# Early starts for x, weight parts and turned rows in a two-block transformer kernel on one Trainium2 core

## The chip, the cores and the metric

The kernel runs on one core of a Trainium2 chip. The metric is the device time of one execution in microseconds; a kernel is run several times and the median counts. In the profile PE is TensorE, DVE is VectorE, ACT is ScalarE, POOL is GpSimd and SP is the engine that only issues DMAs. PEld is TensorE's weight load, which overlaps its matmuls.

## The reference

256 tokens of width 1024 pass through a first block of two layers and then through a second block. Layer 0 mixes with neighbourhood attention (8 heads) and latent attention (8 heads), layer 1 with dilated attention (16 heads in three groups); each is followed by a squared-ReLU MLP of width 4096. The second block mixes three branches (a gated linear recurrence, 8 causal heads, 4 heads over a memory) and ends with a gated feed-forward of width 3072. Cut to what matters:

```python
for layer in range(DEPTH):                      # DEPTH = 2
    xn = rms_norm(x, norm_mix[layer])
    x = x + (even_mixer if layer % 2 == 0 else odd_mixer)(xn, ...)
    x = x + sq_relu_mlp(rms_norm(x, norm_mlp[layer]), mlp_w1[layer], mlp_w2[layer])
x = rms_norm(x, norm_final)
# second block: xn = rms_norm(x, mix_norm_gain); h = xn @ w_in
# x = x + (sum over 3 branches of sigmoid(gate) * (branch @ w_branch)) @ w_out
# x = x + (gelu(conv(xn @ w_gate)) * (xn @ w_up)) @ w_down ; out = rms_norm(x)
```

## The kernel before

All work is written out by hand as one program per engine: the functions `tensor`, `scalar`, `vector`, `gpsimd` and `sync` each issue their engine's instructions in a fixed order, and named events (a semaphore and a count, `tell` and `at`) tie them together. An instruction that waits holds up everything behind it on its engine.

**Weights.** The plan lists 192 slabs of weights, mostly 1024 rows by 256 columns. `sync` loads slab n into `raw` (5 buffers) once the product of slab n-5 is done. Every fp32 product is made of three fp32r products, so each slab is split: ScalarE writes the high part `whi` (`high`, L985; 3 buffers, free again when the product of the slab three before it is done), and the low part `wlo = raw - whi` is written by VectorE (`low`, L1387) or, for slabs that `pooled` names, by GpSimd in four pieces (L2071). `ahead(n)` on each engine means: make the part of slab n+2. Activations are split in the same way: `XH`/`XL` for the normed x (`gained`), `OH`/`OL` for the attention output (`outputs`), `GH`/`GL` (parts of `HH`, `HL` in the profile) for the blended branches. TensorE multiplies hi by hi, lo by hi and hi by lo (L520, or L540 and L556, which go by chunks of x). Slab numbers: IN2 = 122, BLENDS = 134, OUT2 = 152 (two slabs of w_out by rows, 152 and 153, then two halves, 154 and 155), ODO = 86 (w_o of layer 1, slabs 86 to 89), and slab 90 is the first of the second MLP.

**The head.** `x` comes in as rows in two halves of 512 columns. TensorE transposes it in four chunks (`turn_in`, L592), VectorE copies each chunk from PSUM to `XT` (L1577), ScalarE scales it to `XH` (L1017), VectorE makes `XL` (L1425). The gain `mixgain` has its own small transpose (L742), and VectorE's queue copies its result before it copies x. `keep_busy(n)` (L736) issues n matmuls of ones for the clock of TensorE. Behind the chunks VectorE makes the low parts of slab 0 (`first_low`, L1567), slab 1, sums squares, and makes slab 2 (L1387).

**Attention.** Heads are units; stage s of `attend` starts the scores of unit s, and finishes the values of unit s-3 and the transposes of the probabilities of unit s-2. Outside layer 1's dilated heads two units go as a pair. VectorE takes the maxima, then `softmax` scales the exponentials in `SN` (L1474) for TensorE's transposes (L661), and `probs` copies turned rows from PSUM to `PT` (L1482, odd units; ScalarE does the even ones) for the value products (L690). In layer 0, stages 5 to 8 also turn the memory rows (`turn_in(("mem", ...))`), whose PSUM banks come free when `memory_low` has written the low parts `HL` (L1657). PSUM has 8 banks, handed out in turn, so a bank waits for the reader of its use 8 before.

**Between the stages.** At the end of layer 1's mixer, stage 34 yields the last `OL` (L1492); then slab 89 gives four pieces that VectorE adds to `XT` (`onto_natural`, L1517). The first chunk of the next product needs `XH` of the first piece. In the second block's input product VectorE computes two chained norms (`factors`), while ScalarE waits for them (`both mean`, L1255). In its last blend stage (s = 14) ScalarE writes the high parts of the four blended pieces (L1285) behind VectorE's sums (L1926, L1928, L1932).

## Time and profile before

| what | value |
|---|---|
| median of 3 runs | 1252.59 us (1250.91 to 1252.92) |
| the profiled execution's own time | 1252.58 us |
| its span, first to last instruction | 1250.8 us |
| TensorE busy | 1232.5 us, 99% of the span |
| VectorE busy | 819.0 us, 65% |
| ScalarE busy | 620.3 us, 50% |
| GpSimd busy | 275.0 us, 22% |
| granted clock of TensorE, mean | 0.996 |

The profiled execution lies within 0.01 us of the median, and 1.8 us are outside its span. Busy time of TensorE is so near the span that only its gaps and the stretches at a lower clock can be won back without taking work away. In a row of the timeline the columns are start and duration in us, engine, line, operation, output and inputs, number of instructions merged, and in brackets the idle time in front and what ended it.

### The profile page before, as it was taken

Reading aid. Unit: us, or ns where it says so; the run is one execution under the profiler, and the core shown is the slowest. Engines: PE = TensorE matmul, PEld = TensorE weight load, DVE = VectorE, ACT = ScalarE, POOL = GpSimd, SP = SyncE. Lnnn points to the kernel's source line nnn. Section 1 sums busy time; section 2 is a strip of 40 time slices with the busy share of each in tenths; the row PEclk is TensorE's granted clock in tenths of the full one; section 3 lists DMA queues with packets and bytes.
Section 4 is the critical chain, followed back from the end, with each engine's and each line's share of the span. In section 5 each row is a group of like instructions: output and inputs, shape, how many; then the busy total and the mean of one; then the engine's idle time right before and its main releaser. Section 6 shows DMA issues by size and latency. Waiting matters only on the chain.

```text
span 1250.8 us, 23346 instructions
## 1 busy us (share of the span) xinstructions
PE 1232.5 (99%) x10005; PEld 1188.4 (95%) x10005; DVE 819.0 (65%) x1093; ACT 620.3 (50%) x772; POOL 275.0 (22%) x208
## 2 busy tenths in 40 slices
PE   8999999999999999999999999999999999999998
PEld 8978899999999999999999999999999999999986
DVE  6778666655574667666877755497876467656643
ACT  5565455543344454545555553336566435444442
POOL 2500010000021202020310000289211476434100
PEclk9999999999999999999999999999999999999999
DMA  9542455555576555554355555555544455555551
GB/s 277 175 135 102 135 169 178 193 172 199 169 240 212 172 183 172 165 190 144 103 169 174 198 170 197 172 177 172 173 163 141 137 184 169 180 189 171 188 185 65
DMA packets 188693, 214.48 MB, mean 171 GB/s; under 512 B 5243, under 2 KB 170430, under 8 KB 188590
## 3 DMA queue, kind: packets, MB, share of 16 engines
q1 hardware_dynamic: 183182, 205.11, 50.3%
q10 hardware_dynamic: 5216, 7.42, 2.0%
q8 instruction: 79, 1.29, 0.4%
q0 software_dynamic: 192, 0.46, 0.1%
q14 instruction: 24, 0.20, 0.1%
HBM read 205.63 MB, written 1.05 MB: 165 GB/s over the span
## 4 chain that ended last, share of the span: by engine, by line
PE 86%; DVE 3%; ACT 2%; issue 1%; POOL 1%; ACTq 0%; DVEq 0%; POOLq 0%
PE ps L520 76%; PE ps L690 2%; PE ps L556 2%; PE ps L653 2%; PE ps L661 2%; ACT whi L985 1%; POOL wlo L2071 1%; DVE wlo L1387 1%; DVE XT L1517 0%; PE ps L890 0%; DVE HL L1932 0%; DVE BIG L1928 0%; DVE XL L1425 0%; ACTq L1210 0%; ACT XH L1017 0%
## 5 line engine op out<-in xcount | busy, mean ns | idle before, releaser
L1387 DVE TENSOR_TENSOR wlo<-raw,whi 128x2048 fp32r<-128x2048 f32 (+1 forms) x155 | 360.6, 2329 | 203.7 <-ACT whi L985 203.5
L520 PE MATMUL ps<-XH,whi 128*128 128x256 f32 x1592 | 451.6, 285 | 0.0
L520 PE MATMUL ps<-XH,wlo 128*128 128x256 f32 x1592 | 448.4, 283 | 1.6 <-POOL wlo L2071 1.1
L985 ACT ACTIVATE whi<-raw 128x2048 fp32r<-128x2048 f32 (+1 forms) x189 | 359.4, 1906 | 182.5 <-PE ps L520 162.1
L520 PE MATMUL ps<-XL,whi 128*128 128x256 f32 x1592 | 448.1, 283 | 0.0
L520 PEld LDWEIGHTS ps<-XH,wlo 128*128 128x128 f32 x1592 | 304.4, 192 | 2.3 <-POOL wlo L2071 1.3
L520 PEld LDWEIGHTS ps<-XH,whi 128*128 128x128 f32 x1592 | 304.3, 192 | 1.2 <-issue 1.0
L520 PEld LDWEIGHTS ps<-XL,whi 128*128 128x128 f32 x1592 | 304.3, 192 | 0.0
L2071 POOL TENSOR_TENSOR wlo<-raw,whi 128x512 fp32r<-128x512 f32 x136 | 179.8, 1357 | 322.7 <-ACT whi L985 322.6
L520 PE MATMUL ps<-HL,whi 128*128 128x256 f32 x640 | 175.6, 284 | 0.0
L520 PE MATMUL ps<-HH,whi 128*128 128x256 f32 x640 | 175.6, 284 | 0.0
L520 PE MATMUL ps<-HH,wlo 128*128 128x256 f32 x608 | 172.9, 284 | 2.6 <-POOL wlo L2071 2.6
L520 PEld LDWEIGHTS ps<-HL,whi 128*128 128x128 f32 x640 | 121.4, 193 | 0.0
L520 PEld LDWEIGHTS ps<-HH,whi 128*128 128x128 f32 x640 | 121.4, 193 | 0.0
L2137 POOL TENSOR_TENSOR TB<-TB,BIG 128x512 f32<-128x512 f32 x24 | 40.2, 1674 | 365.9 <-DMA TB<-TA 365.9
L520 PEld LDWEIGHTS ps<-HH,wlo 128*128 128x128 f32 x608 | 117.4, 193 | 2.8 <-POOL wlo L2071 2.8
L1047 ACT ACTIVATE SN<-SN,stat 128x512 f32<-128x512 f32 (+2 forms) x64 | 38.3, 600 | 102.0 <-DVE stat L1459 96.6
L520 PE MATMUL ps<-whi,XH 128*128 128x256 f32 x256 | 73.1, 286 | 0.0
L520 PE MATMUL ps<-wlo,XH 128*128 128x256 f32 x256 | 72.5, 283 | 0.1
L520 PE MATMUL ps<-whi,XL 128*128 128x256 f32 x256 | 72.4, 283 | 0.0
L1089 ACT ACTIVATE HH<-TB 128x512 fp32r<-128x512 f32 x32 | 20.3, 633 | 74.3 <-DVE TB L1547 74.3
L520 PE MATMUL ps<-OH,whi 128*128 128x256 f32 x192 | 56.1, 292 | 0.0
(242 smaller groups left out, 1763.3 us busy)
## 6 DMA issues: line engine op xcount, KB each, us to landing
raw<-in_mlp_w_dram SPq DMA_DIRECT2D x64, 1024.0 KB, 5.2
raw<-in_od_w_in_dram SPq DMA_DIRECT2D x36, 1024.0 KB, 5.5
raw<-in_w_in_dram SPq DMA_DIRECT2D x24, 1024.0 KB, 5.2
raw<-in_w_ffn_gate_dram SPq DMA_DIRECT2D x12, 1024.0 KB, 5.0
raw<-in_w_ffn_up_dram SPq DMA_DIRECT2D x12, 1024.0 KB, 5.0
raw<-in_w_ffn_down_dram SPq DMA_DIRECT2D x12, 1024.0 KB, 4.9
raw<-in_ev_w_in_dram SPq DMA_DIRECT2D x6, 1024.0 KB, 11.6
TB<-TA ACTq DMA_DIRECT2D x96, 64.0 KB, 4.1
```

The costliest lines, as they stand in the source:

```text
L520: m = pe.matmul(to, l[c][a], r[c][b], start=first and k == 0, stop=last and k == 3 * n - 1)
L556: i = pe.matmul(b[n][:, m * S:m * S + S], h[a], x[c][z], start=m == c == a == z == 0, stop=m == 1 and c == 7 and z == 1)
L653: m = pe.matmul(banks[u][:, lo:hi], l, r, start=start, stop=stop)
L661: m = pe.transpose(b[:, to:to + P], SN[:, u % 3, of:of + P], ident[:, :])
L690: m = pe.matmul(b[p0:p0 + n, a:z], v, PT[:, u % 3, lo:hi], start=start, stop=stop)
L985: act.activation(whi_of(n), raw_of(n), ACT.Copy, scale=1.0).then_inc(*tell(s_whi, ("whi", n)))
L1047: m = act.activation(SN[:, u % 3, lo:hi], src[:, lo:hi], ACT.Exp, bias=stat[:, u % 3, k:k + 1], scale=-1.0 if biased else 1.0, accum_out=s ...
L1089: act.activation(HH[:, 512 * j:512 * j + 512], TB[j % 2][:, :], ACT.Copy, scale=1.0).then_inc(*tell(s_xhi, ("hhi", layer, j)))
L1387: dve.tensor_tensor(wlo_of(n), raw_of(n), f32(whi_of(n)), ALU.subtract).then_inc(*tell(s_wlo, ("wlo", n)))
L2071: m = pool.tensor_tensor(lo[:, v], r[:, v], f32(hi[:, v]), ALU.subtract)
L2137: pool.tensor_tensor(z, z, twice(RP[:, S:512]), ALU.mult).then_inc(*tell(s_pool, ("sine", k)))
```

## The change

It edits the order of work on TensorE, ScalarE and VectorE in seven places. (1) In the head TensorE turns x's first two chunks ahead of `mixgain`, with 10 filler matmuls for 12; ScalarE's queue issues the DMA of the gain rows before that of the identity. (2) The high parts of x's last chunk are written by VectorE (new `first_high_parts`), and ScalarE makes both halves of slab 0's high part one chunk earlier. (3) In attention with paired units VectorE copies the turned rows before the softmax, not after it. (4) The low part of slab 90 moves on VectorE from behind stage 34 to the end of stage 33, and (5) that of slab 91 behind the second of the four last pieces. (6) The high part of slab 125 moves on ScalarE ahead of its wait for `both mean`. (7) The high part of slab 154 moves ahead of the last two blended pieces.

```diff
@@ tensor
-            keep_busy(3)
+            keep_busy(5)
+            for c2 in range(2):
+                turn_in(("x", c2), [xrow[:, t, :] for t in range(2)], ("x", 0), c2)
             b = bank(("mixgain",))
             once.wait_ge(*at("mixrows"))
-            once.wait_ge(*at("ident"))
             pe.transpose(b[:, 0:16], rows_[0:16, 2, :], ident[0:16, 0:16]).then_inc(*tell(s_product, ("product", "mixgain")))
-            keep_busy(4)
-            for c2 in range(4):
-                if c2 == 2:
-                    keep_busy(2)
-                turn_in(("x", c2), [xrow[:, t, :] for t in range(2)], ("x", c2 // 2), c2)
+            keep_busy(2)
+            for c2 in range(2, 4):
+                turn_in(("x", c2), [xrow[:, t, :] for t in range(2)], ("x", 1), c2)
             keep_busy(3)
@@ scalar
+            act.dma_start(rows_[0:16, 2, :], A["norm_mix"].rearrange("l (c p) -> (l c) p", p=P)).then_inc(*tell(s_mix, "mixrows", by=16))
             act.dma_start(ident[:, :], A["c_ident"]).then_inc(*tell(s_ident, "ident", by=16))
-            act.dma_start(rows_[0:16, 2, :], A["norm_mix"].rearrange("l (c p) -> (l c) p", p=P)).then_inc(*tell(s_mix, "mixrows", by=16))
...
-            for c2 in range(4):
+            for c2 in range(3):
                 for c in (2 * c2, 2 * c2 + 1):
                     gained("mix0", c, gain("mix0", c), ("taken", "x", c2))
-                if c2 % 2:
-                    first_high(c2 // 2)
+                if c2 >= 1:
+                    first_high(c2 - 1)
...
             for n in range(12):
-                ahead(IN2 + n)
+                if n != 1:
+                    ahead(IN2 + n)
                 if n == 0:
                     root("n4", 1, cols=True)
+                    ahead(IN2 + 1)
                     once.wait_ge(*at("both mean"))
...
                     branch(4)
+                    ahead(OUT2)
                     branch(5)
...
-            for k in range(2):
-                ahead(OUT2 + k)
+            ahead(OUT2 + 1)
@@ vector
                 for u in begun(first, n, s):
                     maxima(u)
+                paired = kind_of(first)[0] != DIL
+                if paired and 0 <= s - 2 < n and not act_turns(first + s - 2):
+                    probs(first + s - 2)
                 for u in begun(first, n, s - 1):
                     softmax(u)
-                if 0 <= s - 2 < n and not act_turns(first + s - 2):
+                if not paired and 0 <= s - 2 < n and not act_turns(first + s - 2):
                     probs(first + s - 2)
...
+            def first_high_parts(c2):
+                once.wait_ge(*at(("taken", "x", c2)))
+                for c in (2 * c2, 2 * c2 + 1):
+                    dve.tensor_scalar(XH[:, c, :], XT[:, c, :], gain("mix0", c), None, ALU.mult).then_inc(*tell(s_dve, ("xhi", "mix0", c)))
+
...
-                if c2:
+                if c2 in (1, 2):
                     first_gained(c2 - 1)
+            first_high_parts(3)
+            first_gained(2)
             first_gained(3)
...
-            for k in range(4):
-                ahead(ODO + k)
+                if s == 33:
+                    ahead(ODO + 2)
             for j in range(4):
                 onto_natural(ODO + 3, j)
-                for c in (2 * j, 2 * j + 1):
-                    gained("mlp1", c, gain("mlp1", c))
+                if j == 1:
+                    ahead(ODO + 3)
+                for i in ((), (0, 1), (2,), (3,))[j]:
+                    for c in (2 * i, 2 * i + 1):
+                        gained("mlp1", c, gain("mlp1", c))
```

How this moves instructions, at the three places that matter most. First VectorE in layer 0's attention, stages 7 to 8 (`OL` output of a pair, softmax of a pair, `PT` the copy of turned rows, `HL` the memory's low parts, `SQ` a sum). Before:

```order
L1492 TENSOR_TENSOR OL<-ps,OH 128x256
L1471 RECIPROCAL stat<-stat 128x2
L1474 TENSOR_SCALAR SN<-SN,stat 128x256 x2
L1471 RECIPROCAL stat<-stat 128x2
L1474 TENSOR_SCALAR SN<-SN,stat 128x256 x2
L1482 COPY PT<-ps 128x512
L1657 SCALAR_TENSOR_TENSOR HL<-ps,V,HL 128x256 x2
```

And changed:

```order
L1493 TENSOR_TENSOR OL<-ps,OH 128x256
L1483 COPY PT<-ps 128x512
L1472 RECIPROCAL stat<-stat 128x2
L1475 TENSOR_SCALAR SN<-SN,stat 128x256 x2
L1472 RECIPROCAL stat<-stat 128x2
L1475 TENSOR_SCALAR SN<-SN,stat 128x256 x2
L1668 SCALAR_TENSOR_TENSOR HL<-ps,V,HL 128x256 x2
```

The copy to `PT` has moved ahead of the pair's softmax; the same swap is made at 12 places, 7 in layer 0 and 5 in the second block.

Second VectorE at the end of layer 1's mixer (`XT` adds a piece of slabs 88 and 89, `OL` is the last attention output, `wlo` low parts of slabs 90 and 91, `XL` low parts of x). Before:

```order
L1492 TENSOR_TENSOR OL<-ps,OH 128x128
L1517 TENSOR_TENSOR XT<-XT,ps 128x2x8x16 x4
L1492 TENSOR_TENSOR OL<-ps,OH 128x128
L1387 TENSOR_TENSOR wlo<-raw,whi 128x2048 x2
L1517 TENSOR_TENSOR XT<-XT,ps 128x2x8x16 x2
L1425 SCALAR_TENSOR_TENSOR XL<-XT,V,XH 128x256 x2
L1517 TENSOR_TENSOR XT<-XT,ps 128x2x8x16 x2
```

And changed:

```order
L1493 TENSOR_TENSOR OL<-ps,OH 128x128
L1521 TENSOR_TENSOR XT<-XT,ps 128x2x8x16 x2
L1388 TENSOR_TENSOR wlo<-raw,whi 128x2048
L1521 TENSOR_TENSOR XT<-XT,ps 128x2x8x16 x2
L1493 TENSOR_TENSOR OL<-ps,OH 128x128
L1521 TENSOR_TENSOR XT<-XT,ps 128x2x8x16 x4
L1388 TENSOR_TENSOR wlo<-raw,whi 128x2048
L1426 SCALAR_TENSOR_TENSOR XL<-XT,V,XH 128x256 x4
L1521 TENSOR_TENSOR XT<-XT,ps 128x2x8x16 x2
```

One low part now stands ahead of the last `OL`, the other behind the second piece of slab 89, and the first piece is added with no low part between it and `OL`.

Third ScalarE at the last blend stage (`HH` are the high parts of the four blended pieces, `whi` those of the slabs). Before:

```order
L1065 ACTIVATE OH<-ps 128x256
L985 ACTIVATE whi<-raw 128x2048 x2
L1285 ACTIVATE HH<-BIG 128x512 x4
L985 ACTIVATE whi<-raw 128x2048 x3
L1017 ACTIVATE XH<-XT,V 128x256 x2
```

And changed:

```order
L1064 ACTIVATE OH<-ps 128x256
L984 ACTIVATE whi<-raw 128x2048 x2
L1286 ACTIVATE HH<-BIG 128x512 x2
L984 ACTIVATE whi<-raw 128x2048
L1286 ACTIVATE HH<-BIG 128x512 x2
L984 ACTIVATE whi<-raw 128x2048 x2
L1016 ACTIVATE XH<-XT,V 128x256 x2
```

The high part of slab 154 has moved from behind the fourth blended piece to behind the second. The order of GpSimd's and SP's instructions is unchanged.

## Rows read from the trace of the kernel before

**Rows 1.** Windows: busy of PE, PEld, DVE, ACT, POOL; then TensorE's granted clock.

```profile
90.00:93.40 3.40, 3.25 (x15) 2.21 (x16) 2.19 (x6) 1.62 (x5) 0.00 (x0) 0.51 0.00 0
1025.50:1028.60 3.10, 3.10 (x14) 3.10 (x15) 0.00 (x0) 0.00 (x0) 3.10 (x3) 0.50 1.00 366
```

**Rows 2.** Timeline of the head and up to the first attention wait.

```profile
6.31 1.91 PE L592 MATMUL ps<-ident,BIG 128*128 128x128 f32 x8
7.41 0.69 DVE L1577 COPY XT<-ps 128x512 f32<-128x512 f32 x1 [2.69 <-PE ps L592]
...
13.31 2.35 DVE L1567 TENSOR_TENSOR wlo<-raw,whi 128x1024 fp32r<-128x1024 f32 x2
...
24.82 0.19 PEld L520 LDWEIGHTS ps<-wlo,XH 128*128 128x128 f32 x1 [0.30 <-DVE wlo L1387]
...
43.40 0.63 PE L661 MATMUL ps<-ident,SN 128*128 128x128 f32 x4 [0.85 <-DVE SN L1474]
```

**Rows 3.** Landings of ident (issued 0.7), x's first two (0.7, 1.2), slab 1 (3.6).

```profile
DMA to landing us min/median/max: 3.2/3.2/3.2
...
DMA to landing us min/median/max: 3.0/3.2/3.4
...
DMA to landing us min/median/max: 9.6/9.6/9.6
```

**Rows 4.** Waits in the first 30 us: total, times, longest.

```profile
PE ps L540 <- ACT whi L1102: 1.4, 2, 0.8
```

**Rows 5.** Timeline of layer 0's attention, stages 7 and 8.

```profile
88.06 0.62 DVE L1474 TENSOR_SCALAR SN<-SN,stat 128x256 f32<-128x256 f32 x2
...
89.31 0.68 DVE L1482 COPY PT<-ps 128x512 f32<-128x512 f32 x1
...
90.14 1.98 PE L690 MATMUL ps<-PT,BIG 128*64 128x256 f32 x8 [1.31 <-DVE PT L1482]
...
93.93 0.87 DVE L1657 SCALAR_TENSOR_TENSOR HL<-ps,V,HL 128x256 fp32r<-128x256 f32 x2
```

**Rows 6.** The critical chain behind it: start, us, what.

```profile
94.24 5.74 PE ps L520 x48
```

**Rows 7.** Timeline of the end of layer 1's mixer and the MLP's start.

```profile
617.05 1.11 DVE L1517 TENSOR_TENSOR XT<-XT,ps 128x256 f32<-128x256 f32 x2 [0.28 <-PE ps L520]
...
620.34 0.29 DVE L1492 TENSOR_TENSOR OL<-ps,OH 128x128 fp32r<-128x128 f32 x1 [0.26 <-ACT OH L1065]
620.54 4.49 DVE L1387 TENSOR_TENSOR wlo<-raw,whi 128x2048 fp32r<-128x2048 f32 x2
...
626.73 1.19 PE L556 MATMUL ps<-XH,whi 128*128 128x256 f32 x8 [0.63 <-ACT XH L1017]
...
639.57 0.38 PE L520 MATMUL ps<-XH,wlo 128*128 128x256 f32 x1 [0.54 <-DVE wlo L1387]
```

**Rows 8.** Timeline of the second block's input product.

```profile
824.86 0.42 ACT L1255 ACTIVATE RS<-RS 128x258 f32<-128x258 f32 x1 [4.91 <-DVE RS L1835]
...
827.23 18.07 POOL L2071 TENSOR_TENSOR wlo<-raw,whi 128x512 fp32r<-128x512 f32 x13 [2.56 <-ACT whi L985]
...
832.72 0.39 PE L520 MATMUL ps<-XH,wlo 128*128 128x256 f32 x1 [1.07 <-POOL wlo L2071]
```

**Rows 9.** Timeline of the last blend stage and the output product.

```profile
1002.13 12.33 POOL L2071 TENSOR_TENSOR wlo<-raw,whi 128x512 fp32r<-128x512 f32 x8 [1.85 <-ACT whi L985]
...
1008.10 1.81 DVE L1932 TENSOR_TENSOR HL<-BIG,HH 128x512 fp32r<-128x512 f32 x1 [2.42 <-ACT HH L1285]
...
1011.64 0.63 ACT L1285 ACTIVATE HH<-BIG 128x512 fp32r<-128x512 f32 x1 [3.65 <-DVE BIG L1928]
...
1018.58 0.69 DVE L1932 TENSOR_TENSOR HL<-BIG,HH 128x512 fp32r<-128x512 f32 x1 [0.77 <-ACT HH L1285]
...
1020.42 15.37 POOL L2071 TENSOR_TENSOR wlo<-raw,whi 128x512 fp32r<-128x512 f32 x12 [5.95 <-ACT whi L985]
...
1025.50 0.58 PE L520 MATMUL ps<-HH,wlo 128*128 128x256 f32 x1 [2.58 <-POOL wlo L2071]
```

## The prediction, made before the changed kernel was run

> **What bounds the kernel now.** I read the page first. TensorE is busy for 99% of the span (the table above), so it is the bound nearly everywhere. A reordering can only win its idle time, or time in which it runs at the lower clock. So next I went through TensorE's granted clock in windows. It stands at full rate except in two stretches inside the kernel: 90.0 to 93.4 us, and 1025.5 to 1028.6 us [rows 1], where it is 0.5, which is 1.2 of 2.4 GHz. Both begin just behind a gap of TensorE: 1.31 us in front of 90.14 [rows 5] and 2.58 us in front of 1025.50 [rows 9]. A gap there costs its own length and then half of the stretch behind it. Last I read the timeline around each wait of TensorE. The pitch of its matmuls with 256 columns is 5.74/48 = 0.12 us [rows 6].
>
> The sum is made against the profiled execution's own time, 1252.58 us, which is the median of the runs (1252.59) to 0.01 us.
>
> **The head (edits 1 and 2): 0.15 us, between -0.3 and 0.4.** It looks like a large edit and is worth little, because VectorE's chain decides when the head ends. TensorE waits 0.30 us at 24.82 for slab 2's low part on VectorE, and then 0.85 us at 43.40 for VectorE's softmax [rows 2]; being earlier in front of those only makes them longer. VectorE works without a gap from x's second chunk to `first_low` at 13.31. So I ask when that chain starts. Now the transposes of x start at 6.31 and the first copy follows 1.1 us later, at 7.41 [rows 2]. Changed, they start when x's first half is in: its second DMA is issued at 1.2 and lands 3.4 later, so 4.6; ident, now second on ScalarE's queue, lands at about 1.2 + 3.2 = 4.4 [rows 3]. Eight transposes at the low rate take about 1.7 us of those 1.91 [rows 2], so `mixgain` is turned at 6.35. VectorE's queue has its copy in front of x's, so the first x copy starts at about 6.85, 0.56 earlier than 7.41. Of that the chain loses again: two `tensor_scalar` that ScalarE did before, 0.53 us (two of this form take 0.62 with overlap at 88.06 [rows 5]). `first_low` starts near 13.15 in place of 13.31. The chain can't gain more than about 0.4 us, however early x is: slab 1 lands at 3.6 + 9.6 = 13.2 [rows 3] and ScalarE's high part of it (1.9 us) is then ready at 15.2, while VectorE's low part of slab 1 starts at 15.6 now. If x or ident lands half a microsecond later, the edit costs 0.3 us. TensorE itself wins its two waits for slab 0's high part, 1.4 us [rows 4], and gives them back at slab 2, where its wait becomes about 1.3 us.
>
> **Turned rows first (edit 3): 1.9 us, between 0 and 3.0.** At stage 8 TensorE stops for 1.31 us until VectorE's copy `PT`, 89.31 to 89.99, which stands behind the softmax of a pair, two groups of 0.72 us (a reciprocal, then the scaling, the first at 88.06) [rows 5]. Placed first, the copy starts at 87.87 and ends at 88.55, before TensorE is through with its scores at 88.8. The wait goes, and with it the reason for the low clock: 3.4 us at half rate cost 1.7 us [rows 1]. Together 3.0 us. What is late next? The softmax of the first of the pair, now done at 89.3, is needed at 89.8. Then the PSUM bank for the second block of slab 10 must be freed by `HL`, at 93.93 now [rows 5]. It stands behind VectorE's maxima, which come 1.3 us earlier, so it ends near 93.5 and not at 94.8, and TensorE, which arrives at about 92.8, waits for it. Before, the 48 matmuls of slab 10 end at 99.98 [rows 6], so they begin near 94.0, and the second block, 12 matmuls on, near 95.4. So 95.4 - 93.5 = 1.9 us are won. The other 11 places have TensorE's next use of the softmax behind a slab of 48 matmuls, 5.7 us (stages 3 and 5: behind latent products), which covers a copy of 0.68; I cost them at nothing.
>
> **Slabs 90 and 91 (edits 4 and 5): 0.6 us, between -0.5 and 1.2.** Changed, slab 90's low part (4.49/2 = 2.2 us) stands behind stage 33's adds, which end at 618.16, and so in front of stage 34's adds (1.1 us) and the last `OL`. `OL` ends at 620.63 [rows 7], and TensorE's matmul on it follows within 0.1 us. Now it ends near 618.2 + 2.2 + 1.1 + 0.2 = 621.7: a new wait of 1.07 us. Against that VectorE adds the first piece of slab 89 as soon as TensorE has it, near 622.9, and not behind two low parts near 625 [rows 7], so `XH` is ready at 625.0 and the MLP starts when TensorE is through with slab 89. That was 625.94, where it lost 0.79 us to 626.73 [rows 7]; changed it is 627.0. Through four chunks this is 0.28 us later than before. Then ScalarE and VectorE, with the pieces added 0.8 us earlier, have the parts of slab 92 at 638.6, and the second loss, 0.89 us from slot to slot in front of 639.57 (0.54 of it idle [rows 7]), is gone. 0.79 + 0.89 - 1.07 = 0.6 us.
>
> **Slab 125 (edit 6): 1.2 us, between 1.0 and 1.3.** ScalarE idles 4.91 us until 824.86 for `both mean` [rows 8], and slab 125's high part stands behind it. In front of it, it is done at 821.8, so GpSimd goes on from slab 124's low part at 824.7 without a pause, and not at 827.23. Its four pieces take about 5.5 us, until 830.2; TensorE needs them at 831.5 and now gets them at 832.7 [rows 8]. The idle time is 1.07; with the slot, 1.2.
>
> **Slab 154 (edit 7): 4.1 us, between 1.5 and 4.3.** GpSimd is done with slab 153 at 1014.46 and then idles 5.95 us until slab 154's high part comes, at 1020.42 [rows 9]. ScalarE writes it only behind the fourth blended piece. Behind the second (1011.64 + 0.63) it runs 1012.3 to 1014.2; its buffer is free then, since slab 151's product ends two slabs of 5.76 us ahead of slab 154's first matmuls at 1022.7, near 1011.2. GpSimd's pieces go from 1014.5 to 1019.7 at 1.28 each (15.37/12), or 1020.6 at 1.54 (12.33/8) [rows 9], and TensorE needs them at 1022.8. The third piece is ready only near 1015, so ScalarE isn't late for it. The wait, 2.6 us, goes, and 3.1 us at half rate, worth 1.5 [rows 1]. Slab 155's low part follows on GpSimd at 1020.4 to 1025.6 and is needed at 1028.5.
>
> By the rows the work of GpSimd and VectorE on the same stretch slows both: the same subtraction takes 1.81 us with GpSimd at work and 0.69 us without [rows 9]. The new low part on GpSimd now lies over four such instructions on VectorE (1014.5 to 1019.3), at most 1.12 us each, so the last `HL` moves from 1019.27 to 1021 as a middle value. TensorE needs it at 1023.5, and the bank that the next adds free at 1022.7. Cover enough, so 0 in the sum. The Trainium skill ("SBUF — State Buffer", "Who interferes with whom") speaks against the edit here: two such engines share one port pair under an exclusive lock, and the second to issue blocks until the first is done. By that rule each of the four waits out one GpSimd piece (rival B), and the sum would be 5.6 us; by the rows it is 7.95. Rows of 1.81 beside 0.69 agree with waiting for a piece.
>
> **Sum.** 0.15 + 1.9 + 0.6 + 1.2 + 4.1 = 7.95 us; 1252.58 - 7.95 = 1244.6 us. Between TensorE's waits it is never idle for long, so what is won at one place is kept to the end.
>
> **Rivals.**
> A. *The clock.* A half-rate stretch remains or is new. For: the longer gap before slab 2's low part (1.3 us) is as long as the one that ended at 90.14, and edit 3 wins only if the clock stays up. Against: 0.85 us at 43.40 cushions a stretch there. Cost: 1.7 - 0.85 = 0.9 us near 25, or all 1.9 us of edit 3: 1245.5 to 1246.5 us, as one number 1246.2. The Trainium skill ("TensorE: Matmul & The Clock Gate", "What's actually happening") says that hardware throttles the array's clock by how busy it was, so a gap that goes takes its slow stretch along; the two stretches behind gaps agree.
> B. *The port at slab 154.* Four instructions of VectorE each wait a whole GpSimd piece, 4 x 1.28 = 5.1 us. The last adds free their bank at 1025.0 in place of 1019.9, where TensorE needs it at 1022.7: 2.3 us lost, 1246.9 us. Against: pieces of 0.68 that read PSUM are seen without slowing.
> C. *Little is won.* What is gained at one wait is lost at the next, as in the head, because engines other than TensorE set the pace. Against: TensorE has no wait above 0.3 us from 94 to 420 us. Left is slab 125, and 1252.6 - 1.2 = 1251.4 us.
> D. *Slower.* Turned rows first makes the softmax late at the 12 swapped places: VectorE waits for TensorE's transposes (0.45 us), then copies (0.6) before it scales. If nothing covered it, 12 x 1.05 = 12.6 us, with edit 3's gain gone: 1252.6 - 6.05 + 12.6 = 1259.1 us. It ends above the kernel before by over 0.2% from 0.72 us uncovered at each place. For: at stage 8 the cover is only 0.5 us. Against: elsewhere it is 5.7 us.
>
> **Chances.** Forecast, within 1243.2 to 1245.9 us: 0.62. A 0.17. B 0.07. C 0.06. D 0.03. Better than all this 0.05 (no new wait at 621.7 or 93.5). The range 1243.0 to 1247.5 leaves out C, D and part of the rest. A measurement can't tell less than 0.2%, 2.5 us: slower than that 0.03, within it 0.06, faster 0.91.
>
> **What would show it.** Right: no TensorE wait for `PT` near 88.8 but one of about 0.8 us near 93; a full clock in both stretches of rows 2; a new wait for `OL` of about 1.1 us near 619 and none for `XH` behind it; none for GpSimd's `wlo` at the input or the output product; GpSimd's slab 154 directly behind slab 153; in the head a wait of over 1 us for slab 2's low part, and the softmax wait at 43 hardly moved. Wrong: clock rows of 0.5 at other places, or a wait for `HL` or its bank where slab 154 starts.

## The result and the profile after

| | before | changed |
|---|---|---|
| median (range, runs) | 1251.78 us (1250.20 to 1252.92, 8) | 1248.86 us (1247.23 to 1249.13, 8) |
| profiled execution, span | 1252.58, 1250.8 us | 1248.84, 1247.0 us |
| TensorE busy | 1232.5 us | 1231.7 us |
| granted clock, mean | 0.996 | 0.998 |

The changed kernel takes 0.9974 of the time before (95% interval 0.9963 to 0.9985), 2.9 us less by the medians. Forecast were 8 us, to 1244.6 us, and a range that ended at 1247.5 us.

TensorE's instructions stand in nearly the same order in both traces, so the start of one and the same matmul can be subtracted. The table does that at the places where the difference moves; a plus is later than before. Differences are taken before rounding. Each trace is a single execution.

| TensorE's matmul | before | changed | difference |
|---|---|---|---|
| slab 2, first that needs the low part | 24.82 | 25.97 | +1.15 |
| the same slab, 15 matmuls on | 26.71 | 29.32 | +2.60 |
| first attention's transposes, behind the softmax | 43.40 | 45.07 | +1.67 |
| stage 7, behind `HL` | 86.23 | 87.93 | +1.70 |
| slab 10, second block | 95.51 | 95.23 | -0.28 |
| layer 1, values behind `PT` | 430.05 | 430.04 | 0.00 |
| slab 88, first with the last `OL` | 620.68 | 621.85 | +1.17 |
| MLP's first matmul | 626.73 | 627.11 | +0.38 |
| MLP's first `XL` | 628.72 | 629.46 | +0.74 |
| slab 92, first with the low part | 639.57 | 640.03 | +0.47 |
| slab 125, first with the low part | 832.72 | 831.96 | -0.76 |
| gate products of the recurrence | 851.41 | 851.69 | +0.29 |
| slab 154, first with the low part | 1025.50 | 1023.10 | -2.40 |
| 15 matmuls on | 1028.80 | 1024.90 | -3.91 |
| end of the span | 1250.8 | 1247.0 | -3.8 |

The head, the timeline of the changed kernel (for [rows 2]):

```profile
1.17 0.44 ACTq L1105 DMA_DIRECT2D ident<-in_c_ident_dram  x1
...
5.04 1.97 PE L592 MATMUL ps<-ident,BIG 128*128 128x128 f32 x8 [1.50 <-DMA ident<-in_c_ident_dram]
...
7.26 0.17 DVE L1567 COPY V<-ps 128x16 f32<-128x16 f32 x1 [6.27 <-PE ps L743]
7.35 1.28 DVE L1586 COPY XT<-ps 128x512 f32<-128x512 f32 x2
...
13.77 2.35 DVE L1571 TENSOR_TENSOR wlo<-raw,whi 128x1024 fp32r<-128x1024 f32 x2
...
22.58 5.54 POOL L2107 TENSOR_TENSOR BIG<-BW,namask 128x512 f32<-128x512 f32 x3 [22.15 <-DMA namask<-in_c_namask_dram]
22.90 3.02 DVE L1388 TENSOR_TENSOR wlo<-raw,whi 128x2048 fp32r<-128x2048 f32 x1 [0.72 <-ACT whi L984]
...
25.97 0.58 PE L520 MATMUL ps<-wlo,XH 128*128 128x256 f32 x1 [1.70 <-DVE wlo L1388]
...
40.39 0.69 DVE L1688 TENSOR_TENSOR BIG<-ps,RS 128x512 f32<-128x512 f32 x1 [3.59 <-PE ps L520]
```

The transposes of x begin 1.3 us earlier than before, yet VectorE copies x at 7.35, where it stood before (7.41), because the gain's copy is in front of it. `first_low` is 0.46 us later than before, slab 2's low part takes 3.02 us, and TensorE waits 1.70 us for it.

Windows of the changed kernel, columns as in [rows 1]. The stretch at half rate is new at 26 us; the two of [rows 1] are at full rate:

```profile
26.00:29.30 3.30, 3.30 (x15) 3.30 (x16) 2.78 (x5) 3.02 (x3) 3.30 (x4) 0.50 1.05 400
90.00:93.40 3.40, 3.40 (x28) 2.34 (x29) 3.33 (x12) 1.42 (x4) 0.00 (x0) 1.00 0.00 0
1025.50:1028.60 3.10, 3.10 (x28) 3.10 (x27) 2.41 (x4) 1.43 (x3) 3.10 (x3) 1.00 1.09 390
```

Attention of layer 0, timeline (for [rows 5]): the copy is in time, and the bank is waited for instead:

```profile
89.56 0.68 DVE L1483 COPY PT<-ps 128x512 f32<-128x512 f32 x1
...
95.23 0.39 PE L520 MATMUL ps<-OH,whi 128*128 128x256 f32 x1 [0.61 <-DVE HL L1668]
```

The end of layer 1's mixer, timeline (for [rows 7]):

```profile
618.17 2.29 DVE L1388 TENSOR_TENSOR wlo<-raw,whi 128x2048 fp32r<-128x2048 f32 x1
...
621.85 0.39 PE L520 MATMUL ps<-OL,whi 128*128 128x256 f32 x1 [1.09 <-DVE OL L1493]
...
625.67 2.29 DVE L1388 TENSOR_TENSOR wlo<-raw,whi 128x2048 fp32r<-128x2048 f32 x1
627.88 2.71 DVE L1426 SCALAR_TENSOR_TENSOR XL<-XT,V,XH 128x256 fp32r<-128x256 f32 x4
630.51 1.10 DVE L1521 TENSOR_TENSOR XT<-XT,ps 128x256 f32<-128x256 f32 x2
...
640.03 0.39 PE L520 MATMUL ps<-XH,wlo 128*128 128x256 f32 x1 [0.18 <-DVE wlo L1388]
```

The second block's input product (for [rows 8]): GpSimd runs through, and the gate products wait for the convolution's last tap on VectorE:

```profile
819.89 32.89 POOL L2085 TENSOR_TENSOR wlo<-raw,whi 128x512 fp32r<-128x512 f32 x24 [2.74 <-ACT whi L984]
...
847.42 4.22 DVE L1864 SCALAR_TENSOR_TENSOR BIG<-BIG,V 128x255 f32<-128x255 f32 x3
...
851.69 0.65 PE L889 MATMUL ps<-BIG,SN 64*64 64x256 f32 x4 [0.97 <-DVE BIG L1864]
```

The last blend and the output product (for [rows 9]): slab 154's high part stands at 1012.53, GpSimd has no pause, TensorE no wait:

```profile
1002.47 28.33 POOL L2085 TENSOR_TENSOR wlo<-raw,whi 128x512 fp32r<-128x512 f32 x19 [1.86 <-ACT whi L984]
...
1012.53 1.91 ACT L984 ACTIVATE whi<-raw 128x2048 fp32r<-128x2048 f32 x1
...
1019.55 0.94 DVE L1946 TENSOR_TENSOR HL<-BIG,HH 128x512 fp32r<-128x512 f32 x1 [0.77 <-ACT HH L1286]
...
1023.10 0.28 PE L520 MATMUL ps<-HH,wlo 128*128 128x256 f32 x1
```

### The profile page after: what moved, and what is told of

It is laid out like the page before. It is cut to its first block, busy times and chain, and to the rows that moved or that the text cites. A ratio compares the mean times of both kernels' runs of the same rounds, so it can differ in the third digit from the quotient of the medians.

```text
span 1247.0 us, 23334 instructions
## 1 busy us (share of the span) xinstructions
PE 1231.7 (99%) x10001; PEld 1186.9 (95%) x10001; DVE 817.3 (66%) x1095; ACT 618.8 (50%) x770; POOL 280.4 (22%) x208
## 3 DMA queue, kind: packets, MB, share of 16 engines
HBM read 205.63 MB, written 1.05 MB: 166 GB/s over the span
## 4 chain that ended last, share of the span: by engine, by line
PE 86%; DVE 8%; ACT 2%; issue 1%; POOL 1%; DMA 1%; ACTq 0%; DVEq 0%; POOLq 0%
PE ps L520 75%; PE ps L653 3%; PE ps L690 2%; PE ps L661 2%; PE ps L556 2%; DVE BIG L1864 1%; DVE wlo L1388 1%; DVE XT L1514 1%; DVE XL L1426 1%; ACT whi L984 1%; DMA TB<-TA 0%; POOL wlo L2085 0%; DVE XT L1521 0%; DVE BIG L1860 0%; ACTq L1209 0%
## 5 line engine op out<-in xcount | busy, mean ns | idle before, releaser
L2151 POOL TENSOR_TENSOR TB<-TB,BIG 128x512 f32<-128x512 f32 x24 | 46.1, 1921 | 363.0 <-DMA TB<-TA 363.0
```

Source lines behind the costliest of these rows:

```text
L2151: pool.tensor_tensor(z, z, twice(RP[:, S:512]), ALU.mult).then_inc(*tell(s_pool, ("sine", k)))
```

## Experiments

Each was timed beside the kernel before on its chip. The kernel before itself scatters over 2.4 us or more there, and its medians were 1251.05 us (y runs), 1251.29 (w), 1251.57 (x) and 1252.64 (v). So medians of two groups of runs are not quite like for like, and the ratios are the safer comparison (the changed kernel's is 0.9974). Below one microsecond neither can tell, and the place of TensorE in the trace says more, for that one execution.

| run | median (range) | of the time before |
|---|---|---|
| x1_old_head | 1247.89 (1247.46 to 1250.33) | 0.9975 (0.9965 to 0.9985) |
| x2_slab154_only | 1248.20 (1246.95 to 1248.77) | 0.9969 (0.9959 to 0.9980) |
| x3_new_head_only | 1252.65 (1251.67 to 1254.74) | 1.0008 (0.9999 to 1.0017) |
| x4_gates_later | 1246.67 (1246.40 to 1246.92) | 0.9961 (0.9949 to 0.9974) |
| y1_bias_later | 1248.02 (1247.60 to 1248.27) | 0.9971 (0.9959 to 0.9982) |
| y2_low_part_last | 1247.43 (1247.02 to 1247.59) | 0.9965 (0.9953 to 0.9977) |
| y3_old_slabs_90_91 | 1247.19 (1246.67 to 1247.35) | 0.9963 (0.9950 to 0.9975) |
| y4_slab90_on_gpsimd | 1247.35 (1245.84 to 1248.06) | 0.9960 (0.9947 to 0.9974) |
| w1_squares_on_gpsimd | 1251.05 (1248.92 to 1252.17) | 0.9994 (0.9985 to 1.0003) |
| w2_old_head_gates_slab90 | 1245.40 (1245.32 to 1248.45) | 0.9953 (0.9940 to 0.9965) |
| w3_turned_rows_only | 1250.47 (1249.06 to 1253.50) | 0.9994 (0.9985 to 1.0003) |
| w4_all_mended | 1247.72 (1247.24 to 1248.54) | 0.9967 (0.9955 to 0.9980) |
| v1_old_head_mended | 1245.52 (1244.95 to 1245.76) | 0.9941 (0.9928 to 0.9955) |
| v2_x_copied_first_all | 1245.32 (1245.19 to 1245.86) | 0.9942 (0.9930 to 0.9955) |
| v3_edit2_undone | 1246.90 (1246.73 to 1247.65) | 0.9955 (0.9943 to 0.9968) |
| v4_x_copied_first | 1247.27 (1247.00 to 1247.43) | 0.9956 (0.9944 to 0.9969) |

### The head

**x1_old_head, x3_new_head_only.** Edits 1 and 2 undone in the changed kernel, and alone in the kernel before; their diff is above.

> The changed kernel with edits 1 and 2 (the head) undone. Theory (the new head costs TensorE 1.67 us by 43.4, 1.15 of it because slab 2's low part comes later, the rest from a new half-rate stretch behind the longer wait): 1248.9 - 1.7 = 1247.2 us; the trace shows no rate of 0.5 near 26, slab 2's low part at 24.8 and the second block of slab 10 near 93.5, not at 95.2. Rival (a later wait, at slab 10's bank or at 422, swallows whatever the head wins or loses, so the head is worth nothing): 1248.9 us, and the same place after 422.

> The kernel before with edits 1 and 2 alone. Theory (the head costs 1.7 us at 43.4, and nothing up to the wait for PT at 90 takes it back, since VectorE's chain is late with it): 1.7 us over the kernel before. Rival 1 (my term for the head: 0.15 us gained, the half-rate stretch being an accident of one execution): equal to the kernel before. Rival 2 (the wait of 1.31 us for PT shrinks by what TensorE is late): 0.4 us over.

By its median x1 took 1.0 us less than the changed kernel, but by its ratio (0.9975, against 0.9974) nothing less. x3 took 1.0 us more than the kernel before by its ratio, with an interval that just takes in no change. In x1 slab 2's low part is used at 24.97 and slab 10's second block begins at 93.95, 1.3 us earlier than in the changed kernel. In x3 that place is 2.3 us later than before (97.82), the wait for `PT` is 1.31 us as ever, and the distance stays within 0.6 us of that to the end. So by the times the new head costs something between nothing and 1 us, and in these traces no later wait takes back what it lost. The rival of the shrinking wait falls. Of my term the gain isn't seen; that the head is worth about nothing isn't ruled out by the times alone.

**y1_bias_later.** GpSimd's mask additions wait for slab 2's low part.

```diff
+            once.wait_ge(*at(("wlo", 2)))
             mask_bias(0)
```

> The changed kernel, with GpSimd's additions of mask and bias held back until slab 2's low part is done. Theory (0.7 to 1.0 us of the lateness of slab 2's low part is VectorE's subtraction running beside GpSimd: it took 3.02 us there, 2.29 where GpSimd began no earlier): the subtraction takes 2.3 us, TensorE's wait for it falls from 1.70 to 1.0 us and TensorE is 0.7 to 1.2 us earlier at 43.4; 1247.9 us. Rival (the subtraction is slower for another reason, such as the slab's landing or ScalarE's table load): 3.0 us again, no change. A second rival: the additions, 2.7 us later, are themselves late for the scores, and the kernel is slower by up to 2 us.

The timeline of y1:

```profile
22.85 2.29 DVE L1388 TENSOR_TENSOR wlo<-raw,whi 128x2048 fp32r<-128x2048 f32 x1 [0.72 <-ACT whi L984]
...
25.23 7.90 POOL L2107 TENSOR_TENSOR BIG<-BW,namask 128x512 f32<-128x512 f32 x5 [24.79 <-DVE wlo L1388]
```

Same start as in the changed kernel (22.90), 2.29 us in place of 3.02; TensorE's wait is 0.96 us, no rate of 0.5 follows, and TensorE is 1.04 us earlier at 44.02. In the trace the theory holds. The time is 0.8 us lower by the medians, 0.4 by the ratios (0.9971 and 0.9974), and the intervals overlap, so the runs don't tell it. The same instruction in the other traces, with what follows it (y2, v1 and v2, which use the low part last, have no such wait, and w1 and w4 make it earlier):

| run | GpSimd begins | VectorE begins | takes | TensorE waits | half rate behind |
|---|---|---|---|---|---|
| before | 22.48 | 22.47 | 2.29 | 0.1 | no |
| x1 | 22.64 | 22.62 | 2.29 | 0.1 | no |
| w3 | 21.64 | 22.58 | 2.49 | 0.28 | no |
| w2 | 22.55 | 22.87 | 3.02 | 0.81 | no |
| y1 | 25.23 | 22.85 | 2.29 | 0.96 | no |
| v3 | 22.24 | 22.30 | 3.28 | 1.08 | no |
| x2 | 21.75 | 23.36 | 3.28 | 1.17 | no |
| y3 | 21.85 | 22.63 | 2.57 | 1.26 | no |
| v4 | 21.69 | 22.39 | 2.64 | 1.32 | no |
| x4 | 22.32 | 23.00 | 2.67 | 1.35 | no |
| changed | 22.58 | 22.90 | 3.02 | 1.70 | yes |
| x3 | 21.52 | 23.14 | 3.27 | 1.81 | yes |
| y4 | 21.27 | 22.75 | 3.27 | 1.81 | yes |

The wait is that of the matmul; the 0.30 us of [rows 2] is that of the weight load in front of it, which had been idle for 0.2 us longer. Where nothing holds it, GpSimd begins when the mask has landed, at 21.3 to 22.9 us; if that is before VectorE, the subtraction takes 0.2 to 1.0 us more. In the kernel before VectorE was first by 0.01 us in the profiled execution. The order is not tied to the new head: before, x1, x2, w2 and w3 have the old one, and in x2, w2 and w3 the subtraction was slowed all the same.

**y2_low_part_last.** Slab 2's 16 matmuls with the low part come last.

```diff
+                    order = ((0, 0), (1, 0), (0, 1)) if late == "right" else ...
-            tokens(2, x)
+            tokens(2, x, late="right")
```

> The changed kernel, with the 16 matmuls of slab 2 that need its low part issued last, so that 32 others stand in front of the wait. Theory (TensorE's wait and the half-rate stretch behind it are only 0.5 us of the head's loss, since VectorE's chain, which is 1.15 us late, sets the time at 43.4 in any case): no wait and no rate of 0.5 near 26, a wait for the softmax of 0.5 to 2 us instead near 44.5, and 0 to 0.8 us under the changed kernel. Rival (the wait at slab 2 is the whole loss): 1.7 us under the changed kernel, 1247.2 us.

No wait and no half rate near 26. TensorE waits 1.22 us for the softmax at 43.55 instead, 1.52 us earlier than the same place in the changed kernel. The time is 1.4 us under the changed kernel by the medians, 1.1 by the ratios, between the theory's 0 to 0.8 and the rival's 1.7. But in this execution GpSimd began behind VectorE (22.90 and 22.60), and so the chain itself was earlier too: the run shows that the wait moves to the softmax, and not how the loss divides.

**v3_edit2_undone, v4_x_copied_first.** Edit 2 undone; or edit 1 kept with the identity first on its queue and x's first chunk copied ahead of the gain:

```diff
-            b = take(("mixgain",))
-            dve.tensor_copy(V[:, 0:16], b[:, 0:16])...
             for c2 in range(4):
                 b = take(("x", c2))
                 dve.tensor_copy(XT[:, 2 * c2:2 * c2 + 2, :], pair(b[:, :]))...
                 if c2 == 0:
+                    b = take(("mixgain",))
+                    dve.tensor_copy(V[:, 0:16], b[:, 0:16])...
```

> The changed kernel with edit 2 undone: ScalarE makes all high parts of x again. Theory (the two high parts are 0.53 us on VectorE's chain): the low parts of slab 0 and 1 begin 0.3 to 0.5 us earlier, slab 2's low part 0.3 to 0.8, so 0.5 us under the changed kernel's 1248.9 or, without its half-rate stretch, 1247.0. Rival (the copy of the mix gain in front is the cause, and edit 2 is worth nothing): no change.

> The changed kernel with the identity first on ScalarE's queue and x's first chunk copied ahead of the mix gain on VectorE. Theory (these two are what makes VectorE's chain begin at 7.35 and not at 6): the first copy near 5.9, slab 0's low part 0.5 us or more earlier than 13.77, slab 1's bound by its high part near 15.5, 1 us under the changed kernel. Rival (the high parts wait for the mix gain on ScalarE in any case, so that VectorE's low parts of x come no earlier): slab 0's low part at 13.5 or later and under 0.3 us gained.

The timeline of v4:

```profile
5.97 0.69 DVE L1584 COPY XT<-ps 128x512 f32<-128x512 f32 x1 [4.98 <-PE ps L592]
...
13.27 2.35 DVE L1569 TENSOR_TENSOR wlo<-raw,whi 128x1024 fp32r<-128x1024 f32 x2
```

`first_low` begins at 13.14 in v3 and 13.27 in v4, against 13.77. The nine traces with the new head as it is have 13.40 to 13.94, so both lie below all of them and both causes are real; 0.6 and 0.5 us is their size in this pair of traces. The copy of x at 5.97, 1.4 us earlier, is worth only 0.5 at 13.27. The medians are 2.0 and 1.6 us under the changed kernel, more than the chain gained; the wait of 1.70 us and its half rate are missing in both traces.

**w1_squares_on_gpsimd.** The additions of squares on GpSimd, slab 2's high part behind the second square.

```diff
@@ vector
-            for i in range(1, 4):
-                add_square("n0", 0, i, i == 3)
@@ gpsimd
+            for j in range(1, 4):
+                add_square("n0", 0, j, j == 3)
             mask_bias(0)
@@ scalar
             for c2 in range(4):
                 square("n0", 0, c2, x0[c2], ("taken", "x", c2))
-            high(2)
+                if c2 == 1:
+                    high(2)
```

> The changed kernel with the first norm's additions of squares on GpSimd, ahead of its mask additions, and slab 2's high part behind the second square on ScalarE. Theory (VectorE's chain from slab 1's low part over three additions, each waiting for ScalarE, to slab 2's low part sets the head): slab 2's low part is there before TensorE comes, no wait and no rate of 0.5 near 25, the softmax near 43 is at least 1 us earlier than in the changed kernel; 1.5 to 3 us under it where that has the half-rate stretch, 1246.5 us. Rival (GpSimd's additions, slower and in turn with ScalarE, make the first norm late): a wait for the sum of squares near 23 of about 1 us, and no gain.

GpSimd and TensorE in w1, timeline:

```profile
16.30 2.82 POOL L2095 TENSOR_TENSOR SQ<-SQ 128x512 f32<-128x512 f32 x1 [15.87 <-ACT SQ L1000]
20.23 2.94 POOL L2095 TENSOR_TENSOR SQ<-SQ 128x512 f32<-128x512 f32 x1 [1.11 <-ACT SQ L1000]
23.91 1.26 POOL L2095 TENSOR_TENSOR SQ<-SQ 128x512 f32<-128x512 f32 x1 [0.74 <-ACT SQ L1000]
...
26.02 0.73 PE L577 MATMUL ps<-SQ,ones 128*128 128x256 f32 x2 [3.23 <-POOL SQ L2098]
```

The theory fell to the rival: slab 2's low part was ready at 22.0, but the sum of squares was 3.23 us late. The two additions that lie beside VectorE's low parts took 2.82 and 2.94 us, the third alone 1.26. GpSimd pays for the overlap as well. Behind the wait of 3.23 us the rate was 0.5 from 26.6 to 30.0 us, so w1 doesn't show the head without a stretch either.

### Edit 3 and the stretches at half rate

**w3_turned_rows_only.** The diff is above.

> The kernel before with edit 3 alone. Theory (it always wins the 0.4 us that the traces show from 86 to the second block of slab 10, and 1.6 more in those executions in which the wait for PT is followed by a half-rate stretch, less 0.3 lost later near 121): 0.1 to 1.7 us by execution, about 0.7 us under the kernel before, whose own times scatter over 2.9 us. Rival 1 (my term, 1.9 us in every execution): 1.9 us under. Rival 2 (the softmax, now second, is late at the other places): over the kernel before.

It brought 0.8 us by the ratio, not told from nothing by the interval, and not 1.9. One reason shows in x2, which has the old order and the same wait. The timeline of x2, and its window behind the wait:

```profile
91.14 1.08 PE L690 MATMUL ps<-PT,BIG 128*64 128x256 f32 x8 [1.30 <-DVE PT L1482]
```

```profile
92.00:93.00 1.00, 1.00 (x11) 0.84 (x9) 1.00 (x4) 0.59 (x1) 0.00 (x0) 1.00 0.00 0
```

A wait of 1.30 us, and the full rate behind it. From stage 7's scores to slab 10's second block TensorE takes 9.28 us in the profiled execution of the kernel before (86.23 to 95.51), 7.72 us in x2 (87.25 to 94.97) and 7.30 with edit 3. All other traces with edit 3 show 7.29 or 7.30 too. So by these traces edit 3 wins 0.4 us there, and 1.6 more where the stretch follows. But near 121 us, where a product now waits for VectorE's `XT` (L1514), 0.38 us is lost again in w3, 0.39 in w2 and 0.38 in the changed kernel, whether TensorE comes there at 118.5, 119.4 or 120.4; in x2 it is 0.07. Without the stretch edit 3 wins next to nothing up to that place.

### Slabs 90 and 91

**y3_old_slabs_90_91, y4_slab90_on_gpsimd.** Edits 4 and 5 undone; in y4 GpSimd also makes slab 90's low part.

```diff
             if name == "od_o":
                 return n >= ODO + 2
+            if n == W1[1]:
+                return True
```

> The changed kernel with edits 4 and 5 undone. Theory (they cost 0.47 us by 639.6, and the norms behind them on VectorE are late by as much, so it is lost for good): 0.5 us under the changed kernel; the wait for OL is gone, those for XH (0.6) and slab 91 (0.5) are back. Rival (my term: they win 0.6 us): 0.6 us over the changed kernel.

> The changed kernel with edits 4 and 5 undone and slab 90's low part on GpSimd, which idles there for 17 us. Theory (what costs at 620 to 640 is that two low parts of 2.2 us stand on VectorE's path, in whatever order): no wait for OL, the one for XH down from 0.6 to 0.3 or less, slab 91's as before or gone, so 0.8 to 1.3 us under the changed kernel. Rival (the additions to XT and their parts, one after the other over two engines, are the bound, 2.56 us for each piece): XH and slab 91 are waited for as in the kernel before, 0.5 us under the changed kernel.

In y3 TensorE's lead over the changed kernel grows from 1.65 us in front of 620 to 2.17 at slab 92, so edits 4 and 5 cost 0.52 there. In y4 it goes from 0.24 behind (422.90) to 0.81 ahead (639.22); slab 90's low part runs on GpSimd from 615.93 for 5.04 us, and the waits for `OL` and `XH` are both gone; that for slab 92's low part (0.56 us) is as before. Both theories held in the traces. The medians lie 1.7 and 1.5 us under the changed kernel, which cannot come from there alone: y3's profiled execution is 1.8 us ahead at 43.24 already, in the head, which y3 doesn't touch.

### Slab 125 and the gate products

**x4_gates_later.** The gate products and ScalarE's reading one slab later.

```diff
-                if n in (5, 6):
-                    lru_gate(n - 5)
+                if n in (6, 7):
+                    lru_gate(n - 6)
```

> The changed kernel with the recurrence's gate products (and ScalarE's reading of them) one slab later, behind slabs 128 and 129 and not 127 and 128. Theory (edit 6 wins its 1.2 us at 832, and 1.05 of it is lost at 851.7, where the convolution on VectorE is late for the gate products): the wait of 0.97 us there is gone and the time is 1.05 us under the changed kernel, 1247.8. Rival (VectorE's chain behind the convolution is the bound of the whole stage, so that the wait comes back at the scores behind it): 1248.9 us with a new wait between 855 and 905.

No wait over 0.2 us is left between 640 and the end, and the lead over the changed kernel grows from 0.74 us at 429.31 to 2.01 at 863.92, 1.27 us. The rival fell. The time is 2.2 us under the changed kernel by the medians and 1.6 by the ratios; the trace has no stretch in the head either.

### Slab 154

**x2_slab154_only.**

> The kernel before with edit 7 alone. Theory (edit 7 brings its whole term, the wait of 2.6 us and the half-rate stretch behind it, at any arrival time): 4.1 us under the kernel before, and the traces agree with those of the kernel before up to 1022. Rival (it brings less by itself, since in the changed kernel part of it came with the earlier edits): 2.5 us or less.

0.9969 of the time before (0.9959 to 0.9980), 3.9 us, or 2.5 to 5.1. The trace agrees with that of the kernel before by 0.2 us at 430, and is 4.3 us ahead of it at 1024.13 (1028.44 before). The term stands by itself, and the rival (2.5 us or less) falls.

### Together

> The changed kernel with edits 1, 2, 4 and 5 undone, slab 90's low part on GpSimd and the gate products one slab later. Theory (the losses found so far add up: head 1.0, slabs 90 and 91 0.8, gate products 1.2): 1248.9 - 3.0 = 1245.9 us. Rival (they overlap, since what is won early is waited for again later): 1247 us or more.

> The changed kernel with the gate products one slab later, slab 90's low part on GpSimd with edits 4 and 5 undone, and the first norm's squares on GpSimd with slab 2's high part behind the second square. Theory (these mend three losses at three places that have nothing to do with one another): 1248.9 - 1.2 - 0.8 - 2.0 = 1244.9 us. Rival (the head's gain is lost at slab 10's bank or at 422): 1246.5 us.

w2 is the changed kernel without edits 1, 2, 4 and 5, with slab 90's low part on GpSimd and the gate products later: 1245.4 us, where 1245.9 was expected, so within the noise the losses add up. w4 keeps the new head and puts the squares on GpSimd: 2.8 us over its expectation. Nearly all of that is the head, where the sum of squares is waited for 2.50 us at 25.35 and the rate is 0.5 behind it: the softmax is used at 45.64, 0.6 us later than in the changed kernel, where 2.0 us earlier was expected.

v1 and v2 add y1's and y2's edits to w2, v2 with v4's head.

> The changed kernel with edits 1, 2, 4 and 5 undone, slab 90's low part on GpSimd, the gate products one slab later (1245.4 us with these), and in addition GpSimd's mask additions held back until slab 2's low part is done and slab 2's matmuls with the low part last. Theory (a subtraction slowed beside GpSimd and the wait for it are still there with the old head in most executions): no wait for slab 2's low part, the one at 43 near 1 us, 0.5 us under 1245.4. Rival (VectorE's chain, begun at 7.5, sets the time at 43 whatever TensorE does): 1245.4 again.

> As the first of this series, with the new head (edits 1 and 2 kept) in which the identity is first on ScalarE's queue again and VectorE copies x's first chunk ahead of the mix gain. Theory (the new head is lost by what stands in front of VectorE's first copy of x): that copy begins near 5.9 in place of 7.4, slab 2's low part ends 0.3 to 0.8 us earlier than with the old head, 1244.5 us. Rival (slab 1, which lands at 13.0 to 13.6, is the bound of the chain however early x is): within 0.2 us of the first of this series.

Neither is told from w2, so v1's theory (0.5 us under it) and v2's (1244.5 us) aren't borne out: the medians agree to 0.2 us, the ratios (0.9941 and 0.9942, against 0.9953) differ by 1.4 us but their intervals overlap, and in the traces the wait for slab 2's low part becomes one of 1.2 us for the softmax at 43.5 to 44.2. All three beat the changed kernel, by 3.3 to 3.5 us by the medians and 2.6 to 4.1 by the ratios. Which is best isn't shown.

## Why the prediction was wrong

Two terms held (edit 3 in the trace, and slab 154); the three others, forecast at 1.95 us together, lost 1.96 in the traces.

**The head: 0.15 us forecast, 1.67 us lost in the trace, and by the times between nothing and 1.0.** Three steps failed.

The first is "the first x copy starts at about 6.85": it started at 7.35, as the identity landed 3.8 us after its issue at 1.17 and not 3.2. Over all traces it took 3.2 to 3.8 us where it is first on its queue and 3.5 to 4.0 us where it is second, so 3.2 was the best case. VectorE was only 0.18 us ahead at its last copy of x (10.94, before 11.12), its two high parts cost it 0.5 us, and `first_low` stood at 13.77, not 13.15. The forecast's own figures, 0.56 won and 0.53 lost, would have given 13.28. (The transposes took 1.97 us, not 1.7; the granted clock on record there is 1.00, so "at the low rate" isn't shown.)

The second is the subtraction of slab 2, taken at 2.29 us from a trace in which GpSimd wasn't ahead of it; y1 shows that in the changed kernel this cost 0.73 us. Together slab 2's low part came 1.15 us later. But this is in good part the luck of two executions: `first_low` begins at 13.3 to 14.1 us in the six traces with the old head and at 13.4 to 13.9 in the nine with the new one, and the slowed subtraction comes with either.

The third, and the largest, is the half-rate stretch, my rival A. The trace of w2 shows its price. It has the old head, but happens to be like the changed kernel up to 26 us: GpSimd begins at 22.55, VectorE at 22.87 for 3.02 us, TensorE uses slab 2's low part at 25.94. Its wait was 0.81 us, since TensorE came later, and no stretch followed. Its timeline:

```profile
38.93 0.69 DVE L1684 TENSOR_TENSOR BIG<-ps,RS 128x512 f32<-128x512 f32 x1 [2.13 <-PE ps L522]
```

In the changed kernel the same instruction, which waits for TensorE's product, begins at 40.39, and the softmax behind it is used at 45.07 and not at 43.92. So of the 1.67 us the stretch is 1.15 and the later low part 0.52. The cushion of 0.85 us that rival A counted on isn't one for a stretch, because that softmax itself stands behind TensorE's product. Of the five traces with the new head and nothing else changed before 45 us (changed, x3, x4, y3, y4) three have the stretch and use the softmax at 45.07 to 45.61; the two without it do so at 43.24 and 43.74, within the 43.11 to 44.34 of the five with the old head, none of which has a stretch there. So it is rival A (chance 0.17) that came in the head, at 1.15 us and not 0.9: TensorE comes to slab 2's low part at 24.0 to 24.65 us and not at 24.7 to 25.5, waits longer, and some executions then have the stretch. That rests on ten traces.

**Edit 3: 1.9 forecast, 1.95 in the trace** (+1.67 to -0.28), of which 0.28 is gone again by 430. Losses of 0.6 in between, 0.38 of them near 121, where the forecast put the other 11 places at nothing, are offset by 0.3 won at 430. The mechanism was right, the new wait for the bank 0.61 where 0.8 was forecast. The step that failed is the base of the sum, "the profiled execution's own time, 1252.58 us, which is the median of the runs": the profiled execution of the kernel before held a stretch at 90 that another execution with the same wait didn't (x2). Alone the edit is worth 0.8 us by the runs (w3), with an interval that takes in nothing. More runs also put the kernel before at 1251.78, 0.8 us under the execution from which the sum was made.

**Slabs 90 and 91: 0.6 forecast to be won, 0.47 lost.** The wait for `OL` (1.09) and the end of the one for `XH` came as forecast. "With the pieces added 0.8 us earlier" was wrong: slab 91's low part (625.67 to 627.88) stands in front of the first `XL`, so TensorE waits for that (0.36 from slot to slot) and the third piece is added 0.48 us later than before (630.51, before 630.03). At slab 92 0.27 came back, not 0.89. -1.17 + 0.79 - 0.36 + 0.27 = -0.47.

**Slab 125: 1.2 forecast; 1.23 won at 832 and 1.05 lost at 851.** "What is won at one place is kept to the end" failed. VectorE's chain from the norms over the convolution, from 820 on, was no earlier than before: its last tap ends at 851.6, and in the kernel before at 851.2 (846.93 and 4.24 us). There the gate products began at 851.41, just behind that tap: they had no wait, and no cover either. I looked for TensorE's waits and not for places where it is only just in time. x4 gave the gain back.

**Slab 154: 4.1 forecast, 4.20 in the trace, 3.9 alone.** Each step held: the high part at 1012.53 (forecast 1012.3), GpSimd without a pause, the stretch gone. Rival B's loss of 2.3 us didn't come. VectorE's four instructions on `BIG` and `HL` from 1014 on took 1.07, 0.93, 1.07 and 0.94 us beside GpSimd, where the last three took 0.69 each without it, and the last `HL` began 0.97 us later (1019.55), 0.33 of it from in front of the new overlap (1008.43, before 1008.10). The Trainium skill ("SBUF — State Buffer", "Who interferes with whom") has the second of such a pair wait until the first is done; here none of the three waited out a piece of 1.3 us, each lost 0.24 to 0.38, so here the measurement is milder than that rule as rival B applied it, a whole piece for each instruction. At slab 2, with GpSimd's additions of 1.8 us, up to 1.0 us was lost.

In sum -1.67 + 1.95 - 0.28 - 0.47 + 0.18 + 4.20 - 0.16 (a last 0.16 is lost behind 1047) = 3.75 us, the difference of the spans. By the medians it is 2.9 us, because the profiled execution of the kernel before was 0.8 us slower than its median. No rival's number was met: rival A came in the head alone, and the time of 1248.86 us is that together with the losses at 620 and 851, which no rival had.

## What to carry to other kernels

Before an engine that bounds everything is made earlier, look not only at its waits but at the places where it arrives just as its operand does: each caps what is won in front of it, and an edit in front of it wins only up to the cap. A step moved on a second engine delays what follows it in that queue by its whole length; follow it to the next operand that the bounding engine takes. A gain read from one execution, above all one with a half-rate stretch in it, is to be held against the spread of the runs before it is put into a sum. And before a loss is put down to an edit, the same place is to be looked up in every trace there is: two traces that happen to be alike up to that place, as w2 and the changed kernel, separate causes that one pair of before and after can't.

## What the runs showed of the hardware

Behind the head's wait, whether for slab 2's low part or for the sum of squares, the granted clock fell to half in none of the ten traces with a wait of up to 1.35 us and in all five with 1.70 or more (changed 1.70, x3 and y4 1.81, w4 2.50, w1 3.23). Behind the wait for `PT` of 1.30 or 1.31 us it fell in two (before, x3) and not in x2; behind slab 154's of 2.55 to 2.58 us in all three (before, x3, w3). It needn't fall at once. Windows of x3, whose wait ended at 26.46:

```profile
26.00:28.00 2.00, 1.53 (x12) 1.54 (x13) 1.51 (x3) 1.22 (x2) 2.00 (x2) 0.99 1.05 398
28.00:31.50 3.50, 3.50 (x19) 3.50 (x18) 3.47 (x5) 2.17 (x2) 3.50 (x4) 0.52 1.02 397
```

The changed kernel's times lie in two groups, three at 1247.2 to 1247.7 us and five at 1248.8 to 1249.1. By the traces above a stretch costs 1.15 to 1.6 us, which would fit one that comes in some executions. The mean granted clock, which is on record for every execution, points the same way. The kernel before was executed 60 times beside the experiments: the 14 executions with a mean clock of 0.999 took 1249.81 to 1251.15 us, the 19 with 0.996 took 1252.04 to 1254.08. In x1 the two longest executions (1249.92 and 1250.33 us) have 0.998, the six others, up to 1248.35, have 0.999. So how much of an execution runs at the lower clock differs from one to the next, and a good part of the scatter goes with it. At which places isn't on record, since a single execution of each kernel has a trace.

What the head still holds open is how often the stretch comes with the new head and how often with the old one: five traces each are few, and the times leave its cost anywhere between nothing and 1 us.
